# Two activation tiles placed ahead of the squares buffer in SBUF

## The reference, cut to what matters

```python
h = rms_norm(x, norm_mix[l]) * (1.0 + scale_m) + shift_m
z = h @ w_in[l]
...
for l in range(DEPTH_2):
    h = rms_norm_2(x, ng[0])
    x = x + 0.5 * rms_norm_2(swiglu(h, ffn_w1[l, 0], ffn_w3[l, 0], ffn_w2[l, 0]), ng[1])
    h = rms_norm_2(x, ng[2])
    y = mixer_block(h, w_in[l], ...)
    x = x + rms_norm_2(y, ng[3])
    h = rms_norm_2(x, ng[4])
    y = cross_attention(h, rms_norm_2(mem, mem_norm[l]), xattn_q[l], xattn_kv[l], xattn_o[l])
    x = x + rms_norm_2(y, ng[5])
    h = rms_norm_2(x, ng[6])
    x = x + 0.5 * rms_norm_2(swiglu(h, ffn_w1[l, 1], ffn_w3[l, 1], ffn_w2[l, 1]), ng[7])
```

## The kernel before, in words

| tile | start | size |
|---|---|---|
| `raw_weights` | 16,512 | 24,576 |
| `weights_hi` | 41,088 | 16,384 |
| `weights_lo` | 57,472 | 16,384 |
| `x_res` | 73,856 | 8,192 |
| `y` | 82,048 | 8,192 |
| `squares` | 90,240 | 8,192 |
| 23 tiles, `rstd_x` to `sink_exp` (`param_cols`, `ident`, `flip`, `headsum` and others) | 98,432 | up to 115,392 |
| `h_hi` | 115,392 | 8,192 |
| `h_lo` | 123,584 | 8,192 |
| overlays of each stage (`gh`, `hidh`, `mh` start here; `hidl` at 154,304) | 131,776 | |

## Time and profile before

### The profile page before, as it was taken

The page is one execution under the profiler, slowest core; times in us unless marked ns, Lnnn a source line. Parts: engine busy times, 40 slices in busy tenths (PEclk is TensorE's granted clock), DMA queues, the critical chain, the costliest instruction groups (busy, mean ns, idle before and its releaser), DMA issues.

```text
span 2509.6 us, 43811 instructions
## 1 busy us (share of the span) xinstructions
PE 2341.3 (93%) x18041; PEld 2243.3 (89%) x18041; DVE 1716.7 (68%) x2665; ACT 1201.1 (48%) x1811; POOL 136.8 (5%) x114
## 2 busy tenths in 40 slices
PE   6998898999999988999998999999988999998997
PEld 5977898999999987889898998999987889898997
DVE  6656886886664897887555654664896877555663
ACT  2565445764444433555535444444433455535443
POOL 1000000110110012000000110110012000000110
PEclk9998999999999998999999999999997999999999
DMA  8534574667656552345444654656452336443652
GB/s 243 171 110 141 162 250 150 190 184 226 185 170 203 154 162 76 126 128 185 143 144 126 186 185 143 185 174 204 152 160 76 118 123 191 135 145 123 189 179 85
DMA packets 402038, 400.38 MB, mean 160 GB/s; under 512 B 18006, under 2 KB 399304, under 8 KB 401841
## 3 DMA queue, kind: packets, MB, share of 16 engines
q1 hardware_dynamic: 399457, 389.27, 50.3%
q0 software_dynamic: 2384, 8.32, 1.1%
HBM read 396.45 MB, written 1.09 MB: 158 GB/s over the span
## 4 chain that ended last, share of the span: by engine, by line
PE 71%; DVE 19%; ACT 5%; issue 4%; DMA 1%; ACTq 0%; POOL 0%; DVEq 0%; POOLq 0%
PE gemm_ps L842 59%; DVE weights_lo L1413 5%; DVE y L1854 4%; PE misc_ps L970 2%; PE misc_ps L969 2%; PE gemm_ps L845 2%; PE misc_ps L913 2%; DVE mod_partial L1510 1%; PE misc_ps L922 1%; ACT weights_hi L1096 1%; DVE y L1566 1%; ACT e L1219 1%; DVE x_res L1568 1%; ACT h_hi L1171 1%; PE misc_ps L1002 1%
## 5 line engine op out<-in xcount | busy, mean ns | idle before, releaser
L1413 DVE TENSOR_TENSOR weights_lo<-raw_weights,weights_hi 128x1024 fp32r<-128x1024 f32 x704 | 837.6, 1200 | 470.5 <-ACT weights_hi L1096 468.6
L842 PE MATMUL gemm_ps<-h_hi,weights_hi 128*128 128x256 f32 x3664 | 1054.3, 288 | 53.6 <-DVE h_lo L1547 37.3
L1096 ACT CAST weights_hi<-raw_weights 128x1024 fp32r<-128x1024 f32 x704 | 718.8, 1033 | 682.4 <-PE gemm_ps L842 623.6
L842 PE MATMUL gemm_ps<-h_lo,weights_hi 128*128 128x256 f32 x3664 | 1038.3, 283 | 0.0
L842 PE MATMUL gemm_ps<-h_hi,weights_lo 128*128 128x256 f32 x3664 | 1035.9, 283 | 0.0
L842 PEld LDWEIGHTS gemm_ps<-h_hi,weights_hi 128*128 128x128 f32 x3664 | 703.6, 192 | 64.9 <-issue 48.7
L842 PEld LDWEIGHTS gemm_ps<-h_lo,weights_hi 128*128 128x128 f32 x3664 | 703.4, 192 | 3.3 <-issue 2.2
L842 PEld LDWEIGHTS gemm_ps<-h_hi,weights_lo 128*128 128x128 f32 x3664 | 701.2, 191 | 0.0
L842 PE MATMUL gemm_ps<-hidh,weights_hi 128*128 128x256 f32 x880 | 247.8, 282 | 1.5 <-DVE weights_lo L1413 1.5
L842 PE MATMUL gemm_ps<-hidl,weights_hi 128*128 128x256 f32 x880 | 245.9, 279 | 0.0
L842 PE MATMUL gemm_ps<-hidh,weights_lo 128*128 128x256 f32 x880 | 245.7, 279 | 0.0
(11 more groups left out here) (284 smaller groups left out, 2580.6 us busy)
## 6 DMA issues: line engine op xcount, KB each, us to landing
raw_weights<-in_ffn_w_dram SPq DMA_DIRECT2D x256, 512.0 KB, 3.7
raw_weights<-in_w_in_dram SPq DMA_DIRECT2D x200, 512.0 KB, 3.6
raw_weights<-in_w_mod_dram SPq DMA_DIRECT2D x48, 512.0 KB, 5.2
raw_weights<-in_w_up_dram SPq DMA_DIRECT2D x44, 512.0 KB, 4.5
raw_weights<-in_xattn_kv_dram SPq DMA_DIRECT2D x32, 512.0 KB, 4.2
raw_weights<-in_w_out_dram SPq DMA_DIRECT2D x24, 512.0 KB, 4.5
raw_weights<-in_w_down_dram SPq DMA_DIRECT2D x20, 512.0 KB, 4.9
raw_weights<-in_w_branch_dram SPq DMA_DIRECT2D x16, 512.0 KB, 4.5
```

The source lines that it names most:

```text
L842: mm = pe.matmul(ps[:, c, 0:T], w[:, m, kt, c * P:(c + 1) * P], x[:, f, :], start=start, stop=stop_)
L1096: act.copy(WH[s], RAWB[:, u["raw"] % RAW, 0:u["nkt"], 0:u["cols"]]).then_inc(sems["weights_rounded"], 1)
L1413: dve.tensor_tensor(WL[s], RAWB[:, u["raw"] % RAW, 0:u["nkt"], 0:u["cols"]], WH[s], ALU.subtract).then_inc(sems["weights_rest"], 1)
```

## The change

The line that declares `h_hi` and `h_lo` moves from the end of the list of permanent tiles to just ahead of `squares`. No other line differs.

```diff
@@ -563,6 +563,7 @@
     RAWB = sb("raw_weights", [P, RAW, UNIT_KT, COLS])
     WH, WL = sb("weights_hi", [P, SPLIT, UNIT_KT, COLS], F32R), sb("weights_lo", [P, SPLIT, UNIT_KT, COLS], F32R)
     X, Y = sb("x_res", [P, NF, T]), sb("y", [P, NF, T])
+    HH, HL = sb("h_hi", [P, NF, T], F32R), sb("h_lo", [P, NF, T], F32R)
     SQ = sb("squares", [P, NF, T])
     RX, RY, RQ = sb("rstd_x", [P, T]), sb("rstd_y", [P, T]), sb("rstd_q", [P, 2, T])
     RT = sb("rstd_tok", [P, TT])
@@ -576,7 +577,6 @@
     EPS = sb("eps", [P, 4])
     LAM, SINK = sb("neg_lam", [P, LAYERS]), sb("neg_sinks", [P, 8])
     NM, DEN, RD, ES = sb("neg_max", [P, 4]), sb("den", [P, 4]), sb("rden", [P, 4]), sb("sink_exp", [P, 4])
-    HH, HL = sb("h_hi", [P, NF, T], F32R), sb("h_lo", [P, NF, T], F32R)
 
     def overlay(**shapes):
 
```

## The result

The changed kernel takes 2531.26 us (median of 6 runs, 2527.1 to 2534.7), the one before beside it 2510.27 us. The ratio is 1.0081, 95% interval 1.007 to 1.0091: slower by some 20 us, where I had forecast no difference. The profiled execution took 2529.77 us, its span is 2527.9, so 1.9 us lie outside as before.

What follows compares the result with a forecast made beforehand. TensorE was taken to bound the kernel, by matmul count times start distance plus places where it stands while x buffers are prepared. Terms of 0 for matmuls, VectorE/ScalarE and DMA left 2511.45 us, range 2505 to 2518.

Steps and rivals of the forecast that it cites:

- The frame: Whole kernel: matmul count times start distance sets the time; no instruction changes, so only address-dependent instruction times could add terms.
- VectorE, ScalarE and DMA: Instructions and loads on moved tiles: 0 us, within 0.5 us for VectorE and ScalarE and 0.7 us for DMA.
- Matmuls that stream h: 11,472 matmuls of lines 842 and 845: 0 ns each, within 0.4 ns, so 4.6 us more or less.
- The remainders that could matter barely change: Tile starts in SBUF: all stay 32-byte aligned; `h_hi` only goes from 192 to 128 modulo 256.
- The sum: All terms together: 2511.45 + 0 + 0 + 0 = 2511.45 us, bounds 5.8 us either way.
- Who else works: Other engines busy during matmuls: TensorE gives way to none, so by the skill's rule the term is 0.
- Slower, a meeting of addresses: Rival: h between `y` and `squares` costs TensorE slots, 4.5 ns per matmul, 52 us, 2563 us; chance 0.05.
- Faster, more of the short distance: Rival: more matmuls run at 113.5 instead of 118 ns; if all, 52 us, 2460 us; chance 0.04.
- no address chooses between them: The 113.5 and 118 ns distances share line, tiles and clock, so some relation in time picks one.
- The clock: Rival: two more or fewer 1.2 GHz stretches by luck make 5.8 us; chance 0.03 faster, 0.03 slower, with other scatter.

Runs made afterwards that it cites:

- e4: Changed kernel with 64 unused bytes ahead of `weights_hi` and 64 behind `weights_lo`; ratio 1.0046 to the kernel before.
- e9: Changed kernel with 64 unused bytes ahead of `raw_weights`, so h and the weights shift together; ratio 1.0078 to the kernel before.
- e1: Changed kernel with 64 unused bytes ahead of `h_hi` and 64 behind `h_lo`; ratio 0.9985 to the kernel before.
- e12: Changed kernel with 192 unused bytes ahead of `h_hi` and 192 behind `h_lo`; 2468.95 us against 2509.57 for the kernel before, ratio 0.984.
- e8: Changed kernel with 256 unused bytes ahead of `h_hi`; ratio 1.0079 to the kernel before.
- e14: The kernel of e12 run again, unchanged; ratio 0.986 to the kernel before.
- e5: Kernel before with 128 unused bytes ahead of `h_hi`, shifting h and the overlays; ratio 0.9942 to the kernel before.
- e7: Kernel before with 224 unused bytes ahead of `h_hi` and 64 behind `h_lo`; ratio 1.0026 to the kernel before.
- e6: Kernel before with 160 unused bytes ahead of `h_hi` and 192 behind `h_lo`; ratio 1.0037 to the kernel before.
- e17: Kernel before with 128 unused bytes ahead of `squares`, 128 behind it and 128 ahead of `h_hi`; ratio 0.9973 to the kernel before.
- e18: The kernel of e12 with only `squares` moved, 64 unused bytes ahead of it and 128 behind; ratio 0.9858 to the kernel before.
- e13: The kernel of e5 run again, unchanged; ratio 0.9932 to the kernel before.

## Why the prediction was wrong

*The frame* was right: TensorE sets the time, no instruction came or went, and the sum has a term only where an instruction's time depends on its tile's address. VectorE, ScalarE and DMA cost nothing, as put.

*The step that failed* is "Matmuls that stream h": "The cost I take is 0 ns each", with bounds of 0.4 ns. It measured 2.2 ns in the feed-forward parts (117.8 to 120.0) and 2.4 over all (117.55 to 119.92). The rows were read rightly and badly chosen. I compared tiles at different addresses, but `h_hi`, `hidh` and `hidl` all stand at d = 64 from the weights, and in line 845, where the roles are swapped, d is the negative, 192. None of the rows compared has d = 0, so they could not show what d = 0 costs; a bound taken from rows of one class is none for another. The step ahead of it failed with it: "The remainders that could matter barely change" looked at each tile alone, 192 to 128 modulo 256 for `h_hi`. The remainder between the two operands of one matmul went from 64 to 0 (e4, e9).

*The sum.* 10,992 matmuls of line 842 by 2.37 ns are 26.1 us, and 480 of line 845 by 2.56 ns (116.66 to 119.22) are 1.2 us: 27 us. The span grew by 18.3. Both traces hold the same 18,041 matmuls in the same order, so one can read at each of them how far after lags behind before. The lag grows to 18.6 us in the second layer's mixer (the matmul at 1854.83 us before, 1873.43 after), falls to 12.8 us within it (2044.35 and 2057.18), and ends at 18.3. TensorE in that stretch, before and after (length, busy time and matmuls, granted clock, DMA share, GB/s):

```profile
1854.83:2044.35 189.52, 168.14 (x1103) 0.87 0.34 106
```

```profile
1873.43:2057.18 183.75, 165.25 (x1102) 0.92 0.35 107
```

With the granted clock of 0.87 and 0.92, 48 and 31 us of the stretch are at 1.2 GHz; 17 us fewer are worth at most half, an estimate of 8.5 us. The stretch should have lost 1.5 us on h (620 matmuls) and gained 5.8, so of the missing 9 us some 7 are here, and the clock of these two executions is enough for them. That it was the clock is argued from these numbers; no run takes it apart. Another 2 us are missing from 885 to 1217 us of before (1.0 us lost where 1378 matmuls on h make 3.3), where VectorE's lines 1854 and 1413 make up 21% of the chain; that they hide a part of the price is argued too.

*Who else works.* No run shows TensorE giving way to another engine: the four feed-forward parts take 149.81 us each before and 152.05 after, to the last digit. That fits the rule of the Trainium skill, "SBUF — State Buffer", section "Who interferes with whom", that I cited. What doesn't stand is my inference that "by that rule no placement of tiles could slow a matmul". TensorE streams one operand and loads another. The table of that section calls its two read ports for them independent, but here the distance follows where the one operand lies to the other (e4, e9), and the measurement decides.

*The rivals.* "Slower, a meeting of addresses" had the sign, and its threshold of 0.44 ns was rightly named, at a chance of 0.05. Its mechanism, the neighbours `y` and `squares` and the engines at work on them, is wrong: e1 and e12 leave h between them, and h is at 117.55 and 113.88 ns. Its price of 4.5 ns was twice too high. "Faster, more of the short distance" named something real: 113.3 and 117.8 ns are two courses of the same row, both open at d = 192 and, more rarely, at 64. The reading that "no address chooses between them" holds only within one d: at d = 0 nearly no row has either, and the share of the short one is 5% on h at d = 64 and 34 to 88% at 192.

*The clock* does not order the kernels: 0.963 before and 0.961 after, but 0.967 in e8, which is as slow as after, and 0.954 in e12, the fastest.

## What to carry to other kernels

When a kernel's time is a count of matmuls, read the distance between their starts, and for tiles that move work out the difference between the two operands' starts, modulo 256 bytes, before calling a placement free. A comparison across addresses bounds a new placement only if the new relation is among those compared. A few unused bytes ahead of a tile are a cheap trial: here the changed order with 192 on either side of h took 1.6% off the kernel before (e12), and 1.4% when run again (e14).

## What the runs showed of the hardware

A row of fp32r matmuls, 256 columns streamed and 128 loaded for each, runs at the 2.4 GHz level at 120.0 ns per matmul when both tiles start at the same remainder modulo 256 bytes (after, e8, e9). It runs at 117.8 when the streamed one starts 64 later, with 5% of h at 113 (before, e1), and at either 113.3 or 117.8 when it starts 192 later (e5, e12). The period is 256 bytes (e8), and the relation and not the address counts (e4, e9). Swapping the roles swaps the sign: in line 845, where h is the stationary operand, e7 has d = 224, and with 256 columns of the weights streaming the shares are 4, 59, 17 and 20%, the very ones of h streaming at d = 224 in e6.

The columns streamed hardly set the distance. A few matmuls of line 845 stream 128 columns instead of 256, and in the kernel after 14 distances of theirs take 1.56 us, 111.4 ns:

```profile
137.77 0.27 PE L845 MATMUL gemm_ps<-weights_hi,h_lo 128*128 128x128 f32 x1
...
139.33 0.28 PE L845 MATMUL gemm_ps<-weights_hi,h_hi 128*128 128x128 f32 x1
```

Half the columns save 2 to 9 ns of 113 to 120. Each of these matmuls loads 128 columns as the others do, which makes the load a likely bound; no run varies it, and why the distance depends on where the two operands lie is open.

At d = 192 a row keeps the course with which it starts, over 1000 matmuls and more, and the next row may take the other (e5). What picks it is only half known: the order of tiles shifts the odds (2 of 12 against 12 of 12), moving `squares` alone does not turn the one into the other (e17, e18), and the same program can choose otherwise in the next execution (e5 and e13).
